# Attention of the last two row groups: the four exponentials of a head pair regrouped on ScalarE

## The reference

```python
score = where(causal, sum_h w_idx * relu(q_idx @ k_idx), -inf)
idx = top_k(score, 256)                    # keys picked per query
att = q @ k_sel * 64**-0.5 - slopes[h] * dist     # 8 heads, one shared key/value head
p = softmax(where(valid, att, -inf))
out = p @ v_sel
```

## Time and profile before

| | |
|---|---|
| median of the runs | 3270.72 us |
| the profiled execution | 3273.76 us, span 3272.0 us |
| TensorE | 3165.5 us busy, 97% of the span |
| VectorE, ScalarE, GpSimd | 2014.0 us (62%), 1300.1 us (40%), 805.0 us (25%) |
| granted TensorE clock, mean | 0.989 |
| phase C of group three | about 1780 to 1927 us |
| phase C of group four | about 2636 to 2822 us |

### The profile page before, as it was taken

The page is one execution under the profiler, slowest core; times in us unless marked ns, Lnnn a source line. Parts: engine busy times, 40 slices in busy tenths (PEclk is TensorE's granted clock), DMA queues, the critical chain, the costliest instruction groups (busy, mean ns, idle before and its releaser), DMA issues.

```text
span 3272.0 us, 41937 instructions
## 1 busy us (share of the span) xinstructions
PE 3165.5 (97%) x15075; PEld 2618.1 (80%) x15075; DVE 2014.0 (62%) x3449; ACT 1300.1 (40%) x2213; POOL 805.0 (25%) x680
## 2 busy tenths in 40 slices
PE   8997999999999999999999999999999999999998
PEld 7876788788888888878887878886888888788886
DVE  6987358688708447698995862769767588510001
ACT  4336421633237431351112854228675168421111
POOL 3432200165774100011313520000212325111312
PEclk9998999999999999999999999999999999999999
DMA  7973856599893656535555046552555510445554
GB/s 237 299 246 132 307 187 215 193 300 289 289 297 115 245 200 215 216 133 194 194 194 180 14 178 224 206 200 93 212 195 193 201 70 20 174 175 194 194 193 163
DMA packets 178530, 635.98 MB, mean 194 GB/s; under 512 B 11358, under 2 KB 96906, under 8 KB 116777
## 3 DMA queue, kind: packets, MB, share of 16 engines
q1 hardware_dynamic: 164016, 583.05, 51.5%
q10 hardware_dynamic: 14328, 50.42, 3.9%
HBM read 474.04 MB, written 159.38 MB: 194 GB/s over the span
## 4 chain that ended last, share of the span: by engine, by line
PE 77%; ACT 5%; issue 4%; DVE 3%; DMA 1%; POOL 1%; ACTq 0%; DVEq 0%; SPq 0%; POOLq 0%
PE PS L1885 19%; PE PS L1836 15%; PE PS L1838 15%; PE PS L1837 15%; PE PS L2064 3%; PE PS L1859 1%; PE PS L1860 1%; PE PS L1861 1%; PE PS L2086 1%; PE PS L2087 1%; ACT TMP L912 1%; ACT probs L1037 1%; DVE W L1414 1%; PE PS L2117 1%; PE PS L2118 1%
## 5 line engine op out<-in xcount | busy, mean ns | idle before, releaser
L1885 PE MATMUL PS<-WS,HT 128*128 128x512 f32 x2088 | 481.8, 390 | 4.2 <-POOL WS L575 4.2
L1885 PEld LDWEIGHTS PS<-WS,HT 128*128 128x128 f32 x2088 | 392.8, 188 | 86.8 <-issue 5.2
L1836 PE MATMUL PS<-HF,WS 128*128 128x512 f32 x1024 | 398.7, 389 | 1.3 <-ACT TMP L912 0.9
L1838 PE MATMUL PS<-HF,WS 128*128 128x512 f32 x1024 | 398.4, 389 | 0.0
L1837 PE MATMUL PS<-HF,WS 128*128 128x512 f32 x1024 | 398.4, 389 | 0.0
L1431 DVE TENSOR_SCALAR_CACHE_REDUCE flags<-W,cand 128x640 uint8<-128x640 f32 (+9 forms) x272 | 372.5, 1370 | 32.4 <-DVE cand L1466 24.5
L575 POOL TENSOR_TENSOR WS<-RAW,WS 128x1024 fp32r<-128x1024 f32 x116 | 287.1, 2475 | 367.7 <-ACT WS L785 354.9
L1836 PE MATMUL PS<-HT,WS 128*128 128x512 f32 x816 | 321.8, 394 | 0.8 <-POOL WS L575 0.5
L1838 PE MATMUL PS<-HT,WS 128*128 128x512 f32 x816 | 318.4, 390 | 0.0
L1837 PE MATMUL PS<-HT,WS 128*128 128x512 f32 x816 | 318.2, 390 | 0.0
L713 POOL TENSOR_TENSOR TMP<-TMP 128x512 f32<-128x512 f32 x88 | 115.5, 1313 | 786.1 <-ACT TMP L1162 786.1
(11 more groups left out here) (299 smaller groups left out, 6396.1 us busy)
## 6 DMA issues: line engine op xcount, KB each, us to landing
WS<-split_weights_scratch SPq DMA_DIRECT2D x234, 1024.0 KB, 4.8
split_weights_scratch<-WS SPq DMA_DIRECT2D x116, 1024.0 KB, 5.0
W<-split_weights_scratch SPq DMA_DIRECT2D x114, 1024.0 KB, 4.8
RAW<-in_w_in SPq DMA_DIRECT2D x34, 512.0 KB, 6.0
RAW<-in_w_ffn_gate SPq DMA_DIRECT2D x22, 512.0 KB, 6.3
RAW<-in_w_ffn_up SPq DMA_DIRECT2D x22, 512.0 KB, 6.3
RAW<-in_w_ffn_down SPq DMA_DIRECT2D x22, 512.0 KB, 5.7
gate_b_scratch<-TMP ACTq DMA_DIRECT2D x32, 256.0 KB, 5.3
```

What stands on the lines that cost most here:

```text
L1836: mm(PS[:, bank, :], wh, src[:, 0, k, :], start=k == 0, stop=False)
L1838: ins = mm(PS[:, bank, :], wl, src[:, 0, k, :], start=False, stop=k == KD - 1)
L1885: ins = mm(PS[:, 2 * t + half, :], lhs, split(c, w_part)[:, half * 512:(half + 1) * 512], start=first and part == 0 and w_part == 0, stop= ...
```

## The change

In groups three and four ScalarE's order becomes: in turn (i, 0) copy a0, S0 of pair i - 1, copies a1 and a2, S1 of pair i - 1, (copy a3); in turn (i, 1) the copies up to the middle one of the second half, F0 of pair i, the other copies, F1 of pair i. So both second-half exponentials stand in head 0's turn and both first-half ones in head 1's. A pair's exponentials are then counted in the order F0, F1, S0, S1, and TensorE's transposes of the first half wait for two of them instead of three; those of the second half still wait for four. The instructions are the same in number and size. TensorE's, VectorE's and GpSimd's lists are unchanged, but for that count.

```diff
--- before.py
+++ after.py
@@ -1037,12 +1037,26 @@
                         nc.scalar.activation(row, row, ACT.Exp, bias=mx[:, i % held, e:e + 1], scale=-1.0,
                                              accum_out=total).then_inc(exp_done, 1)
 
-                    def second_half(i, e):
-
-                        j = i if e else i - 1
-                        if halved(g) and 0 <= j < PAIRS:
-                            tiles = RT * g + j // (HEADS // 2) + 1
-                            exponential(j, 1 - e, half_tiles(tiles), tiles)
+                    def first_half(i, e):
+
+                        tiles = RT * g + i // (HEADS // 2) + 1
+                        act.wait_ge(s_masked, part(g, i, e, parts_of(g) - 1) + 1)
+                        if e == 0 and i >= held:
+                            act.wait_ge(recip_done, PAIRS * g + i - held + 1)
+                        exponential(i, e, 0, half_tiles(tiles) if halved(g) else tiles)
+
+                    def between(i, e, u, n):
+
+                        if not halved(g):
+                            return
+                        if e == 0 and i > 0:
+                            tiles = RT * g + (i - 1) // (HEADS // 2) + 1
+                            if u == 0:
+                                exponential(i - 1, 0, half_tiles(tiles), tiles)
+                            if u == min(2, n - 1):
+                                exponential(i - 1, 1, half_tiles(tiles), tiles)
+                        elif e == 1 and i < PAIRS and u == max(0, (n - 1) // 2):
+                            first_half(i, 0)
 
                     for i in range(PAIRS + lag):
                         for e in range(2):
@@ -1056,21 +1070,15 @@
                                     act.wait_ge(pt_used, PT_BASE[g] + (len(table) - 3 if moved else k - 3))
                                 nc.scalar.activation(pt_hl(g, k, len(table), 0, w), PS[:, 4 + k % 2, 0:w], ACT.Copy).then_inc(pt_hi, 1)
                                 bc_copy(k - 3)
-                                if u == 0:
-                                    second_half(i, e)
+                                between(i, e, u, len(banks))
                                 if e == 1 and u == 0 and not halved(g):
                                     spread_sums(PAIRS * g + i - lag)
                             if not banks:
-                                second_half(i, e)
+                                between(i, e, 0, 1)
                             if i >= lag and e == 1 and not banks and not halved(g):
                                 spread_sums(PAIRS * g + i - lag)
-                            if i < PAIRS:
-
-                                tiles = RT * g + i // (HEADS // 2) + 1
-                                act.wait_ge(s_masked, part(g, i, e, parts_of(g) - 1) + 1)
-                                if e == 0 and i >= held:
-                                    act.wait_ge(recip_done, PAIRS * g + i - held + 1)
-                                exponential(i, e, 0, half_tiles(tiles) if halved(g) else tiles)
+                            if i < PAIRS and (e == 1 or not halved(g)):
+                                first_half(i, e)
                     for k in range(len(table) - 3, len(table) - 1):
                         bc_copy(k)
                     for j in range(HEADS // 2):
@@ -2056,7 +2064,7 @@
                         if g > 0 and k == 0:
 
                             pe.wait_ge(ny_done, RT * g)
-                        pe.wait_ge(exp_done, exps_to(g, i, 3 if k0 + tiles <= half_tiles(RT * g + i // (HEADS // 2) + 1) else 4))
+                        pe.wait_ge(exp_done, exps_to(g, i, 2 if k0 + tiles <= half_tiles(RT * g + i // (HEADS // 2) + 1) else 4))
                         if PT_BASE[g] + k >= 2:
                             pe.wait_ge(pt_ready, PT_BASE[g] + k - 1)
                         for a in range(tiles):
```

## The result

The changed kernel takes 3303.41 us (median of four runs, 3301.98 to 3304.65) against 3271.18 us of the kernel before on the same chip. The ratio is 1.0097, 95% interval 1.0084 to 1.0109: it is slower by 32 us. The forecast was 3301.

What follows compares the result with a forecast made beforehand. TensorE, busy 97% of the span, was taken as the bound. Pair delays of 16.9 us in group three and 11.9 in group four plus 1.5 for the ends gave 30.3, forecast 3301 us, range 3285 to 3314.

Steps and rivals of the forecast that it cites:

- The loop through F1: Within each pair: last transposes, copy, F1, next a0; F1 still comes last, so a lower count frees nothing in itself.
- First term: b0 waits for S1 behind a2's copy: 1.06, 1.29, 0.37, 0.57 us later at 10, 12, 14, 16 tiles.
- Second term: Last bank's copy and F1 stand behind F0; alone -0.3, +0.2, +0.6, 0 us at 10, 12, 14, 16 tiles.
- the walk: Start-to-start steps through a pair, a2 to next a0: 6.6, 8.16, 8.80, 9.68 us at 10, 12, 14, 16 tiles.
- The mask: VectorE's next score mask at 14 tiles, delayed by S1's later end: about 4.3 us after a2, before 3.35; no extra cost.
- Sum: Group three 16.9 us, group four 11.9, ends +1.5: together 30.3 us more.
- the ends: First and last pairs of the two stages: +1.5 us, estimated between -1 and +4.
- rival 3: In the two stages, more gaps per pair make TensorE's clock fall, up to 24 us more: 3325; 7%.
- Rivals 1, 2 and 4: 1: shorter wait at a0, faster, 3255, 5%. 2: b0's wait hidden, +4, 3275, 4%. 4: nothing changes, 3271, 3%.

Runs made afterwards that it cites:

- everything early: Against the kernel before: S0 behind the copy of a0, S1 behind a1, F0 behind b0, F1 at the end; 3270.90 against 3272.40 us, ratio 0.9991.

## Why the prediction was right

- *The loop through F1.* The bracket in front of a0 names an exponential before and after, and a0 follows F1 by 1.08 at 12 tiles. The lower count freed nothing by itself. It was not the whole reading for every pair: before, no a0 that follows a pair with 11 tiles has a wait in front of it, and three of these four pairs wait 0.24 us in front of b2 instead.
- *First term, b0 waits for S1.* As a time it is right to 0.01 us at all four sizes. In group three it is also the larger cost. In group four it costs next to nothing by itself, 0.14 us in a pair with 14 tiles (8.80 against 8.66) and none with 16 (9.82 in both). There S1 costs through the copy of a3, and the 25 us of S1's place are both effects together.
- *Second term, F1 behind F0.* Right at 10, 12 and 14 tiles. At 16 tiles the walk rightly had b1 wait for the low part of a3, but was 0.14 too small: b1 started 4.62 after a2 (2821.02 - 2816.40), with 0.17 of idle time for that low part, where the walk had 4.51. From the copy of a3 to b1 it took 1.45 us and not some 1.3, and the rest of the walk moved with it. That path belongs to S1's place and not to F0's: at 16 tiles a0 comes 9.83 after a2 with F0 back in head 0's turn. The two terms don't add as separate prices: taken away alone, F0's place gives back 7 us, and S1's place 30.
- *VectorE.* The mask was expected at 4.3 after a2 and came at 4.25, but not for the reason given, S1's later end by way of GpSimd's sum and the reciprocal. With S1 in front of the small copies GpSimd's sum is over 2.41 us after a2, and the mask still starts at 4.26, right behind the low part of a3 and the reciprocal. It is a3's late copy that holds it. b2 did wait for b0's low part and lost nothing by it in the changed kernel (b2 at 6.21, a0 at 8.80). With F0 out of the way it is this wait that keeps a0 at 8.67 and not 8.5.
- *Sum.* Stage three from first to last transposes grew by 19.4 us and stage four by 12.2; the walk had 16.9 and 11.9 with 1.5 for the ends. Pair by pair, from a2 to the next a0, the traces give 15.5 and 12.0. So group three's pairs came out 1.4 lower than the walk, and its last pair, 3.1 us longer from a2 to its last transposes, made up for it: part of how near the forecast came is luck. In group four the last pair was 0.9 longer, as the walk had it, and the start 0.8 shorter. The last pair has no score part to cover S1. In group three its rows, a2 and b0:

```profile
1932.62 0.63 PE L2072 MATMUL PS<-ident,probs 128*128 128x128 f32 x4
...
1935.76 1.08 PE L2072 MATMUL PS<-ident,probs 128*128 128x128 f32 x4 [2.03 <-ACT probs L1037]
```

b0 is 3.14 after a2 there (before 1.40) with 2.03 of idle time, and behind it the clock fell. TensorE alone in the body of the stage and just behind that gap (us, busy, granted clock, DMA share, GB/s):

```profile
1793.00:1905.00 112.00, 93.50 (x655) 1.00 0.04 15
1936.00:1941.00 5.00, 4.45 (x25) 0.67 0.01 3
```

The clock is 1.00 through the pairs, whose waits are up to 1.1 us each, and 0.67 in the 5 us behind the longer gap. So rival 3 had no part in the pairs, and a small one at the stage's end, some 1.3 us of the 3.1: with the new order in group three alone the last pair, with the same gap and the clock at 1.00, was 1.8 longer than before. It seems to have been given back: before, the granted clock was 0.79 in the 8 us after the stage (1927 to 1935), and after the change it was 1.00 where that phase starts. The 31.6 us of the two stages became 30.9 of span.

- *GpSimd* was taken as free. Nearly so: in one pair at 11 tiles, where a mask and a scaling of rows stand in GpSimd's list behind the pair's late sum, TensorE waited for the spread reciprocals:

```profile
1870.26 0.49 PE L2102 MATMUL PS<-ident,attn 128*128 128x128 f32 x2 [0.51 <-POOL attn L623]
```

That is half a microsecond, and that pair's period was 0.9 longer than its neighbours' (10.83 against 9.93).

- *Rivals 1, 2 and 4* are out: no bank got free earlier, the whole was not hidden (S1 behind a1 shows what hidden would look like, +2.5), though b0's wait by itself nearly was in group four, and the lists did change.
- *What it had wrong beside that.* The idle time in front of the transposes for line 1037 rose to 37.1 us (25.2 + 11.9) and not to some 45. At b0 it is 0.8 to 1.1 us in group three, and 0 to 0.4 in group four, where 0.3 to 0.6 was expected. TensorE's busy time rose by 6 us and did not stay. And the lower end of the range, 3285, is half less than 30 us above the kernel before, not a third less.

What stays open: with everything early, a0 came 7.79 after a2 at 14 tiles against 7.75 before, where I had expected a little less than before, and no run separates why.

## What to carry to other kernels

In an in-order list, look at what the next consumer waits for and count everything that stands between its last input and it: the copy, the small copies, the exponential. An instruction is free only as long as it ends before the consumer's cover does: S1, put behind one bank more, brought 25 to 30 us over 32 pairs. And count what it holds back behind it, too. In group four S1's own consumer hardly lost anything; the copy behind S1 came late, and through VectorE's list the loss came back to TensorE one or two banks later. One run that takes away a single wait (S1 in front of the small copies), read for each stage by itself, tells such paths apart. A semaphore count that falls means nothing if the last event is the same one. And when a reordering costs, the walk that explains it also says where the instruction should stand.

## What the hardware showed

Gaps of 0.8 to 1.1 us in front of b0 and 0.5 to 0.7 in front of a0, pair after pair, left the granted clock at 1.00 in group three. One of 2.03 us at the end of the stage was followed by a fall (0.67 over the next 5 us). The length of the gap doesn't decide it: with the new order in group three alone, and with F0 back in head 0's turn, the same place had a gap of 2.04 us, and the 5 us behind it stayed at 1.00 (1935.44 to 1940.44, and 1928.32 to 1933.32). What tells these runs apart was not found. A fall of the same kind had stood just behind the stage before the change (0.79 over 8 us). Length times missing clock is some 1.7 us for either (estimate), so the time that it cost moved more than it grew.
